# Merge, route and experts of a diffusion trunk as one stage over three groups of three tiles

## The reference, cut to what matters

```
gate = sigmoid(h @ w_merge + b_merge)            # 1024 -> 3 x 1024
proj = einsum('bsnm,nmd->bsnd', br, w_branch)    # three branches, 512 -> 1024 each
out  = sum(gate * proj, axis=2) @ w_out          # 1024 -> 1024
x1   = x + g1 * out
h2   = rms_norm(x1, g_norm2) * (1 + sc2) + sh2
# peer: 8 heads, 16 experts of 16384 for each head and token
q = h2 @ w_q                                     # 1024 -> 2048, 16 halves of 128
s = einsum('thpd,hpkd->thpk', q, keys)           # 128 keys per half
top 16 of each half, top 16 of their 256 sums -> ids, softmax -> gw
act = gelu(einsum('tkd,td->tk', u_tab[ids], h2))
y   = rms_norm(x1 + g2 * einsum('tk,tkd->td', gw * act, v_tab[ids]), g_final)
```

## Time and profile before

| | us |
|---|---|
| median of the runs (5087.65 to 5130.64) | 5111.43 |
| profiled execution | 5101.5 |
| its span on the core | 5099.8 |

### The profile page before, as it was taken

How to read it: one execution, slowest core, us unless ns; L and a number is a source line. 1 busy time by engine, 2 the same in 40 slices (tenths; PEclk the granted TensorE clock), 3 DMA queues, 4 the chain that set the end, 5 groups by cost and what they waited for, 6 DMA issues and landing times.

```text
span 5099.8 us, 46619 instructions
## 1 busy us (share of the span) xinstructions
PE 4161.3 (82%) x14534; PEld 2350.7 (46%) x14534; DVE 3046.5 (60%) x6985; ACT 848.6 (17%) x1837; POOL 1850.9 (36%) x1584
## 2 busy tenths in 40 slices
PE   6899978898999998672033334999999999999995
PEld 1455557674444477552033323444444444444442
DVE  0111126443111148899899998877877777665667
ACT  0111103232000010100055443111111111111110
POOL 0000000000000025555433246666555765566653
PEclk9999978559999999886565566999999999999997
DMA  7211115302000268787554458888998988888895
GB/s 279 107 51 48 50 41 136 144 31 110 30 29 29 92 215 284 269 293 288 218 177 185 169 185 310 335 324 327 324 326 293 339 301 338 322 327 313 309 334 221
DMA packets 379339, 1084.51 MB, mean 213 GB/s; under 512 B 38044, under 2 KB 125724, under 8 KB 375968
## 3 DMA queue, kind: packets, MB, share of 16 engines
q0 software_dynamic: 189616, 686.91, 37.4%
q1 hardware_dynamic: 178616, 352.67, 19.3%
q10 hardware_dynamic: 10944, 42.99, 2.1%
HBM read 993.91 MB, written 88.53 MB: 212 GB/s over the span
## 4 chain that ended last, share of the span: by engine, by line
PE 32%; DVE 12%; issue 4%; DMA 2%; POOL 1%; SPq 0%; ACT 0%; DVEq 0%; POOLq 0%
PE ex_ps_a L2082 15%; PE ex_ps_o L2098 15%; DVE ex_ring L2197 3%; DVE ex_dacc L2265 2%; PE ex_ps_t L2052 2%; DMA ex_u<-in_peer_u 1%; POOL ex_ring L2006 1%; DMA ex_ring<-in_peer_u,ids 1%; DVE ex_acc L2204 1%; DVE ex_pk_oh L1439 1%; DVE ex_pk_oh L1441 1%; DVE ex_pk_i L1408 0%; DVE ex_pk_i L1396 0%; DVE ex_heads L1400 0%; DVE ex_e L1443 0%
## 5 line engine op out<-in xcount | busy, mean ns | idle before, releaser
L2006 POOL DMA_INDIRECT ex_ring<-in_peer_u,ids x512 | 679.9, 1328 | 621.5 <-DVE ex_ring L2197 483.4
L2082 PE MATMUL ex_ps_a<-ex_h2t,ex_w_or_g 128*128 128x512 f32 x2048 | 903.9, 594 | 0.0
L2098 PE MATMUL ex_ps_o<-ex_v_or_g,ex_w_or_g 128*128 128x512 f32 x2048 | 899.1, 592 | 0.0
L2006 POOL DMA_INDIRECT ex_ring<-in_peer_v,ids x512 | 598.7, 1169 | 486.1 <-DVE ex_acc L2204 352.6
L2204 DVE SCALAR_TENSOR_TENSOR ex_acc<-ex_ring,ex_wts,ex_acc 128x1024 f32<-128x1024 f32 x512 | 639.0, 1312 | 0.4 <-DVE ex_wts L2215 0.2
L2197 DVE SCALAR_TENSOR_TENSOR ex_ring<-ex_ring,ex_h2g 128x1024 f32<-128x1024 f32 x512 | 613.1, 1251 | 12.2 <-DMA ex_ring<-in_peer_u,ids 11.4
L2098 PEld LDWEIGHTS ex_ps_o<-ex_v_or_g,ex_w_or_g 128*128 128x128 f32 x2048 | 389.1, 190 | 489.8 <-issue 489.6
L2082 PEld LDWEIGHTS ex_ps_a<-ex_h2t,ex_w_or_g 128*128 128x128 f32 x2048 | 381.0, 191 | 431.4 <-issue 431.4
L2277 DVE TENSOR_TENSOR ex_dacc<-ex_dacc,ex_ps_o 128x1024 f32<-128x1024 f32 x128 | 156.0, 1219 | 488.5 <-PE ex_ps_o L2098 488.4
L2068 PE MATMUL ex_ps_o<-ex_dacc 128*128 128x128 f32 x1024 | 203.7, 379 | 241.2 <-DVE ex_dacc L2265 241.2
L1292 PE MATMUL mg_ps_g<-big,mg_ht 128*128 128x512 f32 x864 | 382.1, 595 | 11.5 <-DMA mg_yt<-s_yt 11.5
(11 more groups left out here) (349 smaller groups left out, 5080.9 us busy)
## 6 DMA issues: line engine op xcount, KB each, us to landing
ex_u<-in_peer_u SPq DMA_DIRECT2D x128, 512.0 KB, 8.6
ex_v_or_g<-in_peer_v SPq DMA_DIRECT2D x128, 512.0 KB, 10.0
ex_w_or_g<-s_g SPq DMA_DIRECT2D x64, 512.0 KB, 7.4
mo_w<-in_w_ada SPq DMA_DIRECT2D x12, 2048.0 KB, 7.9
s_g<-ex_v_or_g ACTq DMA_DIRECT2D x4, 4096.0 KB, 11.6
s_g<-ex_w_or_g ACTq DMA_DIRECT2D x4, 4096.0 KB, 15.2
big<-in_w_merge SPq DMA_DIRECT2D x8, 1536.0 KB, 22.0
ml_qkt<-s_qkt SPq DMA_DIRECT2D x18, 512.0 KB, 3.6
```

Of the source, the lines that this page charges most:

```text
L2006: nc.gpsimd.indirect_dma_start(ring[:, n % R, :], None, table[0], bass.IndirectOffsetOnAxis(ap=keep.ids[:, at:at + 1], axis=0)).then_inc(r ...
L2082: mm = nc.tensor.matmul(ps_a[s % 2][:, 0:NTOK], utt[:, s % 2, k, :], h2t[:, k, :], start=(k == 0), stop=(k == DC - 1))
L2098: mm = nc.tensor.matmul(ps_o[v % 2][:, b, :], w[:, slot, i * P:(i + 1) * P], vch[:, slot, b * 512:(b + 1) * 512], start=(c == 0), stop=(c ...
```

## The change

`merge`, `route` and `experts` become one function, `tail`, in one block. Tiles 0 to 8 form three groups of three. Merge, output projection and queries of a group are cut into units (24, 8 and 16, so 144 for three groups). Each unit loads its own piece of the weights into a ring of five places, and SP loads the piece of unit `d + 5` when unit `d` is done. In merge and query units the weights are the stationary operand and the 384 tokens of the group move; the merged sum comes out turned, so neither it nor its transposes go through memory. The bias becomes ACT's bias operand. Three merge units of the next group stand between the output units and the queries of a group. The gate matrix is built in batches of four tokens, its row half on POOL instead of DVE. Which slot (unit) carries which pick, dots and batches is written out in tables. The dense tiles are now 1 to 4, and the gathered ones 0 and 5 to 8, all in one list of 1280 rows, of which 117 dots are written beside the units; the ring has 8 places and there is one accumulator. `g` is read in blocks of eight chunks (2 MB) instead of two. `w_merge` is no longer loaded in `attend`.

```diff
-            for k in range(DC):
-                sp.dma_start(keep.big[:, k, :], T["w_merge"][0, k * P:(k + 1) * P, :]).then_inc(keep.wm_in[k], 16)
-def merge(nc, T, keep):
...
-def route(nc, T, keep):
...
-def experts(nc, T, keep):
-    R = 10
-    GATHER = (1, 6, 7, 8)
-    DENSE = (2, 3, 4, 5)
-    FIRST_ADD = 211
+def tail(nc, T, keep):
+    GROUPS = ((0, 1, 2), (3, 4, 5), (6, 7, 8))
+    GATHER = (0, 5, 6, 7, 8)
+    DENSE = (1, 2, 3, 4)
+    for g in range(NG):
+        units += [("merge", g, j) for j in range(3 if g else 0, NM)] + [("out", g, j) for j in range(NO)]
+        units += [("merge", g + 1, j) for j in range(3 if g + 1 < NG else 0)] + [("query", g, j) for j in range(NQ)]
+    W = 5
+    GC, OCT, BLK, HB = 4, 8, 16, 4
+    R = 8
+    pick_slot = ([40, 42, 44, 46, 48, 50, 52, 53] + [54, 55, 56, 57, 59, 60, 61, 62] + [63, 65, 66, 67, 68, 69, 70, 71]
+                 + [88, 90, 92, 94, 96, 98, 99, 100] + [101, 102, 104, 105, 106, 108, 109, 110] + [128 + 2 * h for h in range(PH)])
+    share_slot = {64: 0, 73: 1, 103: 2, 112: 3}
+    dots_in = {**{s: 3 for s in range(72, 80)}, **{s: 2 for s in range(80, 83)}, **{s: 3 for s in range(83, 88)},
+               **{s: 5 for s in (111, 113, 114, 115, 116, 117, 118, 119)}, **{s: 3 for s in range(120, 128)}, **{s: 1 for s in range(129, 144, 2)}}
+    for s in range(start_of[0], NU + 2):
+        room = {"merge": 2, "out": 1, "query": 1 + s % 2}[units[s][0]] if s < NU else 2
...
+    FIRST_ADD = N0 + 50
@@ tail: SP
+                if kind == "merge":
+                    sp.dma_start(slot[:, 0:D].rearrange("p (k n) -> p k n", k=DC),
+                                 T["w_merge"][0, :, at:at + P].rearrange("(k p) n -> p k n", p=P)).then_inc(into, 16)
...
@@ tail: POOL
+            def hot_rows(n):
+                pool.wait_ge(pk_out, i + 1)
+                if n >= 2:
+                    pool.wait_ge(gm_done, n - 1)
+                for u in range(HB):
+                    last = nc.gpsimd.tensor_scalar(hot[:, n % 2, 0, u, :], keep.iota[:], pickt[i % 2][:, 0, t:t + 1],
+                                                   pickt[i % 2][:, 2, t:t + 1], ALU.is_equal, ALU.mult)
+            for s in range(NU + 2):
+                for n in batches.get(s, []):
+                    hot_rows(n)
+                    while s > pick_slot[0] and sent < dots_before[s + 1] + R:
+                        gather(sent)
@@ tail: PE
+            def merge_unit(s, g, j):
+                pe.wait_ge(unit_in[s % W], arrived[s])
+                if n >= 2:
+                    pe.wait_ge(gate_done, n - 1)
+                for k in range(DC):
+                    mm = nc.tensor.matmul(ps[:, j % 2, 0:GN], wring[:, s % W, k * P:(k + 1) * P], ht[:, k, :], start=(k == 0), stop=(k == DC - 1))
+                if n >= 2:
+                    pe.wait_ge(mult_done, n - 1)
+                for k in range(4):
+                    mm = nc.tensor.matmul(ps[:, 2 + j % 2, 0:GN], wring[:, s % W, D + k * P:D + (k + 1) * P], yt[:, br, k, :], start=(k == 0), stop=(k == 3))
+            def query_unit(s, g, j):
+                for k in range(DC):
+                    mm = nc.tensor.matmul(ps[:, 4 + j % 2, 0:GN], wring[:, s % W, k * P:(k + 1) * P], merged[:, k, :], start=(k == 0), stop=(k == DC - 1))
+            for s in range(NU + 3):
+                for n in batches.get(s - 1, []):
+                    gates(n)
...
@@ tail: ACT
+                nc.scalar.activation(gate[:, br, :], ps[:, j % 2, 0:GN], ACT.Sigmoid, bias=bm[:, br * DC + blk:br * DC + blk + 1]).then_inc(gate_done, 1)
+            def score_rows(g, h):
+                for i, t in enumerate(GROUPS[g]):
+                    if o >= 2:
+                        act.wait_ge(st_sc[o % 2], 16 * (o // 2))
+                    nc.scalar.copy(sc[:, o % 2, :], ps[:, 1 + 2 * (o % 2), 0:2 * P]).then_inc(sc_done, 1)
+                    act.dma_start(T["sc"][t, h], sc[:, o % 2, :]).then_inc(st_sc[o % 2], 16)
@@ tail: DVE
             def add_row(n):
-                dve.wait_ge(used, n - 1)
-                nc.vector.scalar_tensor_tensor(out=acc[k % 2][:], in0=ring[:, n % R, :], scalar=wts[:, k:k + 1],
+                dve.wait_ge(used, n)
+                nc.vector.scalar_tensor_tensor(out=acc[:], in0=ring[:, n % R, :], scalar=wts[:, k:k + 1],
...
+            for s in range(NU):
+                for number, slot in enumerate(pick_slot):
...
+                for n in range(dots_before[s], dots_before[s + 1]):
+                    dot(n)
+                if kind == "merge":
+                    product(g, j)
+                if kind == "out" and j == NO - 1:
+                    for t in GROUPS[g]:
+                        add_mixed(t)
+                    for t in GROUPS[g]:
+                        mean_square(t)
+                    for t in GROUPS[g][0:2 if g + 1 < NG else GT]:
+                        modulated(t)
```

More of the change, by code:

```diff
@@ new lines, in tail @@
+        pickt = [a.rearrange("p (a n) -> p a n", a=3) for a in (merged_or_w[:, 9 * GN:9 * GN + 3 * P], w_or_v[:, W * 1536:W * 1536 + 3 * P])]
+        tot, gw = sb("tl_tot", [P, PH]), sb("tl_gw", [P, PH, TOPK])
+        dots, gelu, wts = (sb(f"tl_{n}", [P, PICKS]) for n in ("dots", "gelu", "wts"))
+        ss = sb("tl_ss", [P, GT, 3])
+        half = sb("tl_half", [P, 1])
+        hold = sb("tl_hold", [P, 2])
+        ps = ctx.enter_context(nc.psum_tensor("tl_ps", [P, 8, 512], F32))
+        ps_o = [ps[:, 2 * b:2 * b + 2, :] for b in range(2)]
@@ new lines, in gates @@
+            def gates(n):
+                pe.wait_ge(a_done, n + 1)
+                pe.wait_ge(b_done, n + 1)
+                if n >= 2:
+                    pe.wait_ge(g_out, n - 1)
+                for i, c in turn_at.items():
+                    if n == c:
+                        pe.wait_ge(pk_out, i + 1)
+                for u in range(HB):
+                    mm = nc.tensor.matmul(ps[:, 6 + n % 2, u * P:(u + 1) * P], hot[:, n % 2, 1, u, :], hot[:, n % 2, 0, u, :], start=True, stop=True)
+                mm.then_inc(gm_done, 1)
@@ new lines, in _ @@
+            act.wait_ge(bm_in, 16)
+            for s in range(NU + 2):
+                if s in share_slot:
+                    i = share_slot[s]
+                    act.wait_ge(exd_in, i + 1)
+                    nc.scalar.activation(exd[i % 2][:, 0:PICKS], exd[i % 2][:, 0:PICKS], ACT.Exp).then_inc(exd_done, 1)
+                if s == pick_slot[PH - 1] + 2:
+                    act.wait_ge(ex_in, 1)
+                    exponentials(0)
+                for n in batches.get(s, []):
+                    if n >= 2:
+                        gate_rows(n - 2)
+                    hot_cols(n)
+                if s - 1 in share_slot:
+                    pick_rows_out(share_slot[s - 1])
+                if s < NU:
+                    kind, g, j = units[s]
+                    if kind == "merge":
+                        sigmoid(g, j)
+                        if g > 0 and j == 1:
+                            turned_h2(GT * (g - 1))
+                        if g > 0 and j == 2:
+                            turned_h2(GT * (g - 1) + 1)
+                            turned_h2(GT * (g - 1) + 2)
+                    elif kind == "query":
+                        queries(g, j)
+                    if s == 1:
+                        key_rows()
@@ L2302, in _ @@
             s = 0
-            for n in range(PICKS, NROW):
+            for n in range(N0, NROW):
                 gi, k = n // ROWS, n % ROWS
```

1274 lines of the change are left out of this document (561 added, 713 removed).

## The result

The changed kernel took 4773.57 us (median of 4 runs, 4748.71 to 4811.09) against 5099.54 (4 runs) of the kernel before: a ratio of 0.937, 95% interval 0.927 to 0.947. The profiled execution took 4789.76, its span 4788.1. I had said 4670; the forecast's sum is 125 short of the profiled execution, and rival A's 4825 is nearer to the median than it.

What follows compares the result with a forecast made beforehand. PE and DVE by turns bound the old kernel; DMA would bind the new loop. 1194 ahead, 1239 stage, 20 start, 2170 loop, 40 end and 2 made 4665, stated as 4670 us; range 4470 to 4860.

Steps and rivals of the forecast that it cites:

- rival A: New stage bound by work beside the units: POOL's instruction at 1.29 us adds 155, 4825 in all; chance 0.20.
- The arithmetic: New stage: PE's matmuls and transposes sum to 1127 us, the same work as before without the waiting.
- the small waits: New stage: PE waits 22 us at its start, 5 each after groups 0 and 1, 22 before the last queries.
- POOL's new work: New stage: POOL's one-hot instruction taken at 0.55 us, between 0.28 and 1.29; slots lose 17 us in all.
- The bound passes from PE to DMA: Loop: DMA's 2153 us exceed DVE's 1992 and PE's 1875, so DMA sets the time.
- DVE sum of 1992: Loop: DVE's dots, adds, dense adds, picks and tile ends total 1992 us, 8% behind DMA.
- the DMA term: Loop: 786 MB at 365 GB/s take 2153 us; with 17 added, 2170.
- What I had named as proof: Loop: DMA share 0.95 or more at some 360 GB/s, chunks every 17 us, PE standing for DVE's dense adds.
- The adds: Loop: with one accumulator each of DVE's 640 adds takes 1.42 us, 909 in all; 800 as lower bound.
- Rival B: Loop: DMA does not bind, DVE's 1992 us set the time; 4490 us in all; chance 0.20.
- Rival C: Loop: gathers landing in up to 17 us make the eight-place ring bind; 5335 us, slower than before; chance 0.06.
- The start: Loop: some 20 us ahead of the rows, as DVE waits for ACT's gelu, which stands behind chunk 1.

Runs made afterwards that it cites:

- e1: Changed kernel with the gate matrix's one-hot rows written by DVE instead of POOL; 4727 us, 0.930 of the kernel before.
- e6: Changed kernel with each gather in the chunk loop bringing 512 of a row's 1024 columns; 4788 us.
- e11: Changed kernel with one wait more: each dot in the loop starts only after the previous dot signalled its end; 4782 us.
- e7: Changed kernel with ten ring places instead of eight in the chunk loop; 4800 us.
- e5: Changed kernel with each chunk's gate product (`weigh`) done by DVE behind a dense add instead of by POOL among gathers; 4803 us.
- e3: Changed kernel loading only the first two of 16 blocks of `g` in the loop; 4742 us, 0.945 of the kernel before.
- e8: Changed kernel with both gate products on DVE and gathers of 512 columns; 4707 us.
- e10: Changed kernel with one-hot rows and gate products on DVE, nine ring places, two accumulators, earlier loop start; 4593 us, 0.905 of the kernel before.
- e2: Changed kernel with `peer_u` chunks loaded earlier at the loop's start, ahead of blocks of `g`; 4813 us, 0.946 of the kernel before.

## Why the prediction was right and wrong

**The stage.** The arithmetic (1127 us of PE; 1140 in e1) and the small waits held: the first wait was 28 us for 22, the one ahead of the last queries 13.5 for 22, and with rows on DVE the stage took 1240 for 1217. The step that failed is "POOL's new work": 0.55 us was taken, nearer to the lower bound, 1.07 and 0.90 measured, and with it some 82 us. That is rival A's mechanism at about half its 155. I had cited the Trainium skill, GPSIMD Engine Reference, "Engine selection", against the move, and had worked wrongly from it: twice DVE's 0.28 gives an estimate of 0.56, my own price, and not half as much again. The trace agrees with neither reading: alone the instruction takes 0.78, 2.8 times DVE's. What is above 0.78 comes with DVE beside it, which I had not priced.

**The loop.** 2190 us were forecast with its start, and 2220 passed from the last gate matmul to the last row (to the end of the span less the 38.6 us of tile ends). The number stood and the step behind it did not. "The bound passes from PE to DMA" is refuted by e6: some 290 MB less changed nothing. What the runs show in its place is DVE and POOL in step, through a ring of eight places: POOL's product stretches a DVE instruction 128 times, DVE's gapless dots stretch gathers, and in picks the ring fills and POOL stands (215 us). The gap between dots is worth 39 us (e11), two places 39 (e7), the product on DVE 13 by itself (e5). That these make up the whole limit is argued and not shown, and the 32 us of e3 stay outside it. My DVE sum of 1992 and POOL sum of 1710 were each made as if the other engine were not there. That the DMA term came to nearly the same length is luck, though DMA is not far off: halving the bytes is worth 3 us in the changed kernel, 55 with the products on DVE (e5, e8) and 83 in e10.

**What I had named as proof** was a DMA share of 0.95 or more, at some 360 GB/s. It came, 0.96 and 359, and proved nothing: e6 has the same time at 0.70. Chunks came every 16.2 us for 17. PE standing for DVE's dense adds did not come (2.7 us).

**The adds** at 1.42 were nearly right (1.39), and so was the end (38.6 for 40). **Rival B** (DMA does not bind) was right in its condition and wrong in its time, since DVE's 1992 could not be reached beside POOL. **Rival C**, the ring, is real but small: two places more give 39 us, and landings stayed at 8 us, far from 15.8. **The start** of the loop was priced too low: 20 us were taken ahead of the rows, and DVE's wait for ACT's gelu alone was 49. Of the 117 us to the first values only 10 come back when the loads are reordered (e2).

**The rest of the 125**: 14 less ahead of the stage, 6 more at its start, 104 more in it, 30 more in the loop, 1 less at the end.

## What to carry to other kernels

A DMA share near 1, with an engine standing for a landing, doesn't show that DMA binds: halve the bytes and look at the time. When work moves from DVE to POOL, price it beside what DVE does in the same microseconds, not by itself, and add what DVE loses; gathers that POOL issues are such work too. Here DVE's dots without a gap were slower for the whole than dots with 0.12 us between them, because another engine's work stood beside them; try such a gap before relying on it, since gathers beside the adds of e10 needed none.

## What the runs showed of the hardware

- A DVE dot of 1024 columns took 1.22 us by itself and 2.54 where a 1.27 us product on POOL fell on it.
- A gather issued by POOL took 0.95 us beside an idle DVE, 1.08 beside adds that wait for each other, 1.98 beside dots without a gap (e8), and mostly 0.94 beside adds into two accumulators (e10).
- The same one-hot instruction on 128 columns came every 0.28 us on DVE and every 0.78 on POOL alone; two on POOL beside dots without a gap took 3.08 and 2.43.
- In e10, over 1900 us, DMA moved 372 GB/s at a share of 0.99. The Trainium skill, DMA: Bandwidth & Descriptors, "Where 436 GB/s comes from", puts memory near 358 for each of the two cores that share it; here one core runs, and this run is above it.
